# A seven-product matrix scheme notes its weight slot as free, and at once lets the next weight form be written out

## The reference, cut to what matters

```python
dq, dk, dv = jnp.split(p[..., c0:c1], 3, axis=-1)      # from p = h @ w_in
...
h2 = rmsnorm(x, norm2_g[l])
gate = jnp.einsum('bsd,df->bsf', h2, w_gate[l])        # D_FF = 2816
up = jnp.einsum('bsd,df->bsf', h2, w_up[l])
x = x + jnp.einsum('bsf,fd->bsd', jax.nn.silu(gate) * up, w_down[l])
```

## Time and profile before

| | |
|---|---|
| times of 3 runs | 3722.06 us median (3717.59 to 3725.05) |
| the profiled execution | 3724.5 us, its span 3722.8 us |
| PE / DVE / ACT / POOL busy in the span | 95% / 58% / 31% / 47% |
| PE busy, 1100 to 1660 us | 544.57 of 560.00 us |
| PE busy, 3086 to 3680 us | 585.99 of 594.00 us |

### The profile page before, as it was taken

How to read it: one execution, slowest core, us unless ns; L and a number is a source line. 1 busy time by engine, 2 the same in 40 slices (tenths; PEclk the granted TensorE clock), 3 DMA queues, 4 the chain that set the end, 5 groups by cost and what they waited for, 6 DMA issues and landing times.

```text
span 3722.8 us, 51933 instructions
## 1 busy us (share of the span) xinstructions
PE 3518.2 (95%) x22042; PEld 2937.1 (79%) x22042; DVE 2152.4 (58%) x2745; ACT 1154.7 (31%) x1919; POOL 1738.0 (47%) x1248
## 2 busy tenths in 40 slices
PE   7999998988999999999898999989999899999998
PEld 6878877877778787877777888777788787877876
DVE  7754566467364545456874466637778355454545
ACT  2122112357222222223122122236666222222223
POOL 4222432639355545555332332533388345545455
PEclk9999999999999999999999999999999999999999
DMA  3101312554201111113111132261222210111011
GB/s 123 36 24 35 142 51 85 183 146 128 82 23 46 57 46 57 46 57 136 41 41 35 35 147 83 99 220 58 69 91 58 80 35 34 68 35 68 35 68 63
DMA packets 79690, 275.82 MB, mean 74 GB/s; under 512 B 9057, under 2 KB 9313, under 8 KB 76900
## 3 DMA queue, kind: packets, MB, share of 16 engines
q1 hardware_dynamic: 70816, 242.25, 19.5%
q10 hardware_dynamic: 8642, 30.24, 2.1%
HBM read 224.23 MB, written 48.23 MB: 73 GB/s over the span
## 4 chain that ended last, share of the span: by engine, by line
PE 72%; DVE 17%; ACT 4%; issue 3%; POOL 3%; DMA 0%; POOLq 0%; SPq 0%; DVEq 0%; ACTq 0%
PE ps L1411 19%; PE ps L1412 19%; PE ps L1413 19%; PE ps L1417 4%; DVE acc L2108 3%; PE ps L1711 2%; PE ps L1681 2%; PE ps L1682 2%; PE ps L1716 2%; DVE tf_lo_p L2107 2%; DVE af_hi_p L2107 1%; ACT wd_hi L1765 1%; DVE af_lo_p L2107 1%; PE ps L1486 1%; DVE px L2107 1%
## 5 line engine op out<-in xcount | busy, mean ns | idle before, releaser
L2692 POOL TENSOR_TENSOR ring_lo<-ring_raw,ring_hi 128x512 fp32r<-128x512 f32 (+1 forms) x356 | 599.6, 1690 | 383.4 <-ACT ring_hi L1765 373.8
L1411 PE MATMUL ps<-a_hi,ring_hi 128*128 128x512 f32 x1472 | 590.9, 401 | 29.4 <-DVE af_hi_p L2107 16.3
L1412 PE MATMUL ps<-a_lo,ring_hi 128*128 128x512 f32 x1472 | 577.9, 393 | 0.0
L1413 PE MATMUL ps<-a_hi,ring_lo 128*128 128x512 f32 x1472 | 577.4, 392 | 0.0
L1411 PEld LDWEIGHTS ps<-a_hi,ring_hi 128*128 128x128 f32 x1472 | 279.0, 190 | 104.0 <-DVE af_hi_p L2107 23.9
L1413 PEld LDWEIGHTS ps<-a_hi,ring_lo 128*128 128x128 f32 x1472 | 278.9, 189 | 60.1
L1412 PEld LDWEIGHTS ps<-a_lo,ring_hi 128*128 128x128 f32 x1472 | 279.4, 190 | 54.4
L2107 DVE TENSOR_TENSOR xres<-xres,ps 128x512 f32<-128x512 f32 x352 | 234.9, 684 | 149.8 <-PE ps L1413 147.6
L1411 PE MATMUL ps<-wd_hi,af_hi 128*128 128x512 f32 x704 | 277.9, 395 | 23.4 <-DVE xres L2107 17.5
L1412 PE MATMUL ps<-wd_lo,af_hi 128*128 128x512 f32 x704 | 276.6, 393 | 0.0
L1765 ACT ACTIVATE ring_hi<-ring_raw 128x512 fp32r<-128x512 f32 (+1 forms) x286 | 180.5, 635 | 309.1 <-PE ps L1413 195.9
(11 more groups left out here) (305 smaller groups left out, 8075.5 us busy)
## 6 DMA issues: line engine op xcount, KB each, us to landing
ring_raw<-w SPq DMA_DIRECT2D x92, 512.0 KB, 3.5
ring_raw<-wgu SPq DMA_DIRECT2D x68, 512.0 KB, 3.7
uq<-q_scr SPq DMA_DIRECT2D x96, 256.0 KB, 4.7
ring_raw<-wd SPq DMA_DIRECT2D x34, 512.0 KB, 3.6
ring_raw<-wo SPq DMA_DIRECT2D x32, 512.0 KB, 3.7
uk<-k_scr SPq DMA_DIRECT2D x6, 2048.0 KB, 10.7
rlf<-wgu SPq DMA_DIRECT2D x20, 512.0 KB, 4.6
xraw<-xt SPq DMA_DIRECT2D x16, 512.0 KB, 7.2
```

The lines of the kernel that those rows point to most:

```text
L1411: pe.matmul(o, ah, bh, start=begin and i == 0, stop=False)
L1412: pe.matmul(o, ah, bl, start=False, stop=False)
L1413: last = pe.matmul(o, al, bh, start=False, stop=end and i == len(pairs) - 1)
L2692: tt = lambda o, a, b, op: pool.tensor_tensor(o, a, b, op=op)
```

## The change

One line: behind `emit("wino", ...)` and the noting of the slot as free, the next weight step is written out at once, ahead of the step that the caller writes next (the gathering of the product's results).

```diff
             f = jobs[n]["forms"][k]
             emit("wino", hf, x, key, p, b, free, f, n, k)
             f["slot"].free = [P(p)]
+            split_next()
```

## The result

The changed kernel takes 3776.31 us (median of 4 runs, 3775.14 to 3779.59); the kernel before, beside it on the same chip, 3723.56 us (3717.59 to 3725.22). The ratio is 1.0145, 95% interval 1.0129 to 1.0161: **slower by 53 us**. The forecast was 3780.

The account below looks back on a forecast made before the run. PE is busy 95% of the span; VectorE, late in freeing bank 0 for b11, makes it wait. Waits 31.5, clock 22.3 and first query and key pair 4 sum to 58 us: 3722 + 58 = 3780, range 3716 to 3798.

Parts of the forecast that it names:

- The first collision: Pairs (g,1): GpSimd's low part of form 6 starts 0.10 us ahead of gu_mul 00, which ends 1.06 us later.
- rival 2: VectorE wins at gu_mul 00: 3764; or at the second gu_mul alone: 3739. Chance 0.17 for both forms.
- The down weights: Pairs (g,1): VectorE's wd_lo ends at 1345.25 instead of 1345.03, +0.22 us for product b22.
- Form 0 and form 1: Next pair's low parts hold af_lo (+0.73) and gu_mul 10; b11 1.75 us later per group, 31.5 us over 18.
- The clock: b11's idle time grows to 2.36 us; half-clock stretches follow, 18 x 0.75 x 1.65 = 22.3 us.
- Rival 1: Same collisions, but PE's clock hardly falls: 3758; chance 0.13.
- The first query and key pair: Low parts of forms 6 and 0 hold VectorE's activation forms, 0 to 2.6 us per half, 2.0 taken: +4.
- Rest at nothing: Pairs (g,0), form 3's copy ahead of the last silu, and later query and key pairs: no cost.
- Rival 3: Faster, 3713: wd_hi ends 0.52 us earlier, if form 6's low part starts after 1338.33 and form 0's behind af_lo; chance 0.11.

Follow-up runs that it names:

- up pairs alone: Early form step written only in the feed-forward up pairs (g,1), the rest as in the kernel before: 3753.35 us, ratio 1.0085.
- gate pairs and form 6: Changed kernel with the early step only in gate pairs (g,0) and, in up pairs, behind product b21: 3734.23 us, ratio 1.0034.
- Gate pairs alone: Early form step written only in the feed-forward gate pairs (g,0), the rest as in the kernel before: 3722.97 us, ratio 1.0000.
- query and key pairs alone: Early form step written only in the query and key pairs, feed-forward pairs as in the kernel before: 3725.85 us, ratio 1.0012.

## Why the prediction came out as it did

**The first collision: right.** The prediction had form 6's low part 0.10 ahead of gu_mul 00, and 1.06 lost; it was 0.08 ahead and the gu_mul took 1.76 for 0.69. All 18 idle times of b11 lie between 2.29 and 2.34, so it went the same way each time, and rival 2 (VectorE wins) did not occur in the changed kernel. Both of its forms were met in part kernels. With gu_mul 00 free (up pairs alone) b11 came 1.0 later per group, with 2.2 us idle, as that rival had worked out (1.1 and 2.2); with gu_mul 10 free (gate pairs and form 6) 0.68 later, 1.3 idle and no stretches (0.7, 1.3, none). So the sums hold away from the forecast too, but for the number of stretches in the first.

**The down weights: right.** Counted from the addition ahead of gu_mul 00, `wd_lo` ended at 7.42 before (1337.61 to 1345.03) and at 7.67 now (1343.80 to 1351.47): +0.25, predicted +0.22. It shows as b22's new wait of 0.26.

**Form 0 and form 1: right, the assumption too.** af_lo took 1.17 (predicted 1.19), the sum started 0.12 ahead of gu_mul 10 (0.11), and b11 came at 13.66 for 11.91 from the same mark: +1.75, the predicted value to the hundredth. From b11 to b11 it is 1.70 per group. The load did come 2 us earlier (form 0's copy 5.49 behind the mark, before 7.59), and form 1's raw weights had landed: its copy started at 1350.62, and GpSimd was busy with form 0's low part until about 1352.6 (0.55 ahead of af_lo's end at 1353.16). The rule of the Trainium skill (SBUF — State Buffer, "Who interferes with whom"), that the issue order decides who blocks, is what the trace shows at all three places, with leads of 0.08 and 0.12 us at the two gu_muls, while af_lo came into a low part that had been waiting since 1350.33; making GpSimd wait turned the same instructions back to 0.69, 0.68 and 0.69.

**The clock: right in mechanism, and the number partly by luck.** Predicted idle time 2.36, measured 2.33; price 1.65, measured 1.60; frequency 0.75, measured 15 of 18 (0.83). The term was 22.3. The 15 stretches cost 24.0, and 22.4 more than before, since the kernel before has one of its own, which the prediction did not take off: three small errors cancel. Its price doesn't follow from its own count either. Ten matmuls where fifteen fit would be 5 x 0.227 = 1.1; but only eight of the ten start inside that window, and 7 x 0.227 is 1.6, as measured. How many stretches an idle time of this length brings, no run fixes: at 2.2 to 2.4 us it was 9 of 17 in one kernel. Rival 1 (3758) fell all the same.

**The first query and key pair: the term that was mis-sized.** I took 2.0 us per half, "the upper part"; PE's wait grew by 1.0 per half (sl_p 10.1 to 12.0). The traces show which instruction it was. Before, GpSimd has three low parts back to back there, now four, form 6's being the last; POOL and DVE before, then now:

```profile
630.97 6.21 POOL L2692 TENSOR_TENSOR ring_lo<-ring_raw,ring_hi 128x512 fp32r<-128x512 f32 x3
638.29 1.22 DVE L2107 TENSOR_TENSOR tf_lo_p<-tf_lo_p,tf_hi_p 128x1024 f32<-128x1024 f32 x1
```

```profile
633.40 8.41 POOL L2693 TENSOR_TENSOR ring_lo<-ring_raw,ring_hi 128x512 fp32r<-128x512 f32 x4
640.73 2.17 DVE L2108 TENSOR_TENSOR tf_lo_p<-tf_lo_p,tf_hi_p 128x1024 f32<-128x1024 f32 x1
```

One activation form of 128x1024 is held for 0.95 us ahead of PE's wait, which grows by 0.94 (5.00 to 5.94). The held subtractions behind it cost PE nothing that shows: the prediction had each of two low parts hold VectorE, and only one did where PE waits. The time of that part alone is 4 us above its own measurement of before with an interval of 1 to 8, so only the waits give the size.

**Rest at nothing: right for the changed kernel.** Gate pairs alone gave 1.0000. The copy of form 3 ahead of the last silu and of the last af_hi, which the prediction put at nothing, is free only under cover: with VectorE's path shortened, the one ahead of the last af_hi costs 23 us. The prediction named the silu for it and not the last af_hi, which is the dangerous one.

**Rival 3 (faster, 3713) was the right reading of what the edit offers.** Its first condition failed by a tenth of a microsecond. The second, that form 0's low part starts behind `af_lo`, failed by 1.66 us in the changed kernel (1350.33 against 1351.99) and by 0.29 in the run of the up pairs alone (1346.02 against 1346.31). And gu_mul 10 needs a third, which the rival did not name: there too GpSimd was ahead, by 0.12. Where all three were made true by three waits, the time was 3708; the gain was larger than the rival's 0.52 per group, 0.82.

The sum was 58 us against 52.7 measured: 31.5 for the waits (measured 30.5 by af_hi_p and rhf), 22.3 for the clock (22.4), 4 for the first pair (1.9). The measured terms add up to 54.8; the 2 us that are left are less than single executions differ by.

## What to carry to other kernels

Where VectorE and GpSimd both work from SBUF, making an instruction of the engine off the critical path ready sooner can take a whole instruction's time from the one on it: compare its new start with the start of each VectorE instruction with two SBUF inputs there, and where it comes out ahead, try a wait that lets the critical engine go first; here it turned a loss of 53 us into a gain of 14. PE's waits at one place add up, and half-clock stretches came with the longer idle time, so two parts that cost 12 and 16 us by themselves can belong to a change that costs 53. A copy with a late input, put ahead of another on an in-order engine, can be free under a cover and cost 23 us once the cover is gone, so it is to be looked at again after each wait that is removed.

## What the runs showed of the hardware beyond the forecast

- Behind b11, idle times of 1.28 to 1.33 us were followed by a half-clock stretch in 0 of 18 cases, of 1.7 to 1.9 us in 1 of 17, of 2.29 to 2.34 us in 15 of 18; those of the run of the up pairs alone, 2.2 to 2.4 us, in 9 of 17. Each stretch took 1.60 us (63.02 against 64.62 per group; 62.33 against 63.93 in the run of the up pairs alone). The length of the idle time alone doesn't decide: in the changed kernel 2.33 us at 1165.21 was not followed by one, and 2.29 us at 1228.23 was; 1.79 us ahead of the b11 at 1657.02 was in the kernel before, and 1.77 us at the same place in the run of the query and key pairs alone was not; 3.11 us at the same place was before (granted clock 0.50 behind it) and not in the changed kernel (1.00). What else decides isn't settled by these runs.
- Held VectorE instructions of 128x1024 end 1.09 us behind the end of GpSimd's low part, twice the 0.55 of one of 128x512: the activation form 641.81 to 642.90, `wd_lo` 1350.38 to 1351.47.
